# Sliding-window attention in chunks of 64 queries with 64x64 score tiles, instead of units of two heads and 128 queries

## The reference

```
CHUNK = 64; WINDOW = 128               # a chunk of queries sees its own chunk and the two before it
s = einsum('...lhgd,...mhd->...hglm', q, k) * HEAD_DIM ** -0.5
s = where(key_pos >= 0, s, -1e30)      # prompt: no keys ahead of the stream
p = softmax(concat([s, sink], -1))[..., :-1]      # one learned sink per head
a = einsum('...hglm,...mhd->...lhgd', p, v)
merged = concat([rms_norm(a, g_a), rms_norm(b, g_b), c]) @ w_out
```

## Time and profile before

| | us |
|---|---|
| median of 3 runs (lowest, highest) | 1426.18 (1425.39, 1429.57) |
| the profiled execution, own time | 1430.02 |
| its span, first to last instruction | 1428.0 |
| PE busy, share of the span | 1376.4, 96% |
| DVE busy | 688.4, 48% |
| ACT busy | 505.5, 35% |
| POOL busy | 213.1, 15% |
| mean granted TensorE clock | 0.982 |

### The profile page before, as it was taken

One profiled execution on the slowest core, in us unless ns is written; L12 is line 12 of the kernel. 1 busy time (PEld: TensorE's weight loads), 2 busy tenths in 40 slices (PEclk: granted clock), 3 DMA queues, 4 the chain that ended last, 5 costly groups with the idle time before them and its releaser, 6 DMA issues.

```text
span 1428.0 us, 24272 instructions
## 1 busy us (share of the span) xinstructions
PE 1376.4 (96%) x10358; PEld 1324.3 (93%) x10358; DVE 688.4 (48%) x1320; ACT 505.5 (35%) x1088; POOL 213.1 (15%) x257
## 2 busy tenths in 40 slices
PE   8999979999999999999999997899999999999996
PEld 8989858999999999999999896599999999999996
DVE  6556783555444444221458487717644444441213
ACT  4223374544232223222433125836532322232220
POOL 6502101520000000011343030124100000001110
PEclk9999988999999999999999999899999999999998
DMA  4412100213222222222222120002222222222211
GB/s 161 163 60 71 45 1 1 104 45 106 87 88 76 89 74 90 84 80 89 75 105 102 47 71 30 1 30 90 89 89 75 89 75 89 81 83 89 74 60 67
DMA packets 33643, 107.96 MB, mean 76 GB/s; under 512 B 4304, under 2 KB 8928, under 8 KB 33536
## 3 DMA queue, kind: packets, MB, share of 16 engines
q1 hardware_dynamic: 31056, 101.26, 20.7%
q0 software_dynamic: 2480, 5.15, 1.1%
HBM read 103.25 MB, written 3.15 MB: 75 GB/s over the span
## 4 chain that ended last, share of the span: by engine, by line
PE 80%; DVE 13%; issue 2%; ACT 2%; DMA 0%; POOL 0%; POOLq 0%; DVEq 0%; ACTq 0%
PE psum L449 25%; PE psum L451 24%; PE psum L450 24%; DVE h_lo L1238 2%; DVE mx L1487 1%; DVE w_lo L1231 1%; DVE x L1286 1%; PE psum L469 1%; PE psum L546 1%; DVE prob L1502 1%; DVE rsq L1373 1%; PE psum L745 1%; PE psum L459 1%; DVE h_whole L1515 1%; PE psum L570 1%
## 5 line engine op out<-in xcount | busy, mean ns | idle before, releaser
L449 PE MATMUL psum<-h_hi,w_hi 128*128 128x320 f32 (+1 forms) x2192 | 660.7, 301 | 5.2 <-DVE hid_whole L1275 3.1
L450 PE MATMUL psum<-h_lo,w_hi 128*128 128x320 f32 (+1 forms) x2192 | 651.2, 297 | 0.0
L451 PE MATMUL psum<-h_hi,w_lo 128*128 128x320 f32 (+1 forms) x2192 | 651.1, 297 | 0.0
L449 PEld LDWEIGHTS psum<-h_hi,w_hi 128*128 128x128 f32 x2192 | 417.5, 190 | 11.0 <-DVE hid_whole L1275 3.5
L450 PEld LDWEIGHTS psum<-h_lo,w_hi 128*128 128x128 f32 x2192 | 417.8, 191 | 2.2 <-issue 1.9
L451 PEld LDWEIGHTS psum<-h_hi,w_lo 128*128 128x128 f32 x2192 | 417.8, 191 | 0.0
L1231 DVE TENSOR_TENSOR w_lo<-raw,w_hi 128x1024 fp32r<-128x1024 f32 x184 | 232.1, 1267 | 337.7 <-ACT w_hi L883 337.6
L883 ACT ACTIVATE w_hi<-raw 128x1024 fp32r<-128x1024 f32 x184 | 192.4, 1050 | 177.1 <-DMA raw<-in_wts 176.8
L449 PE MATMUL psum<-hid_hi,w_hi 128*128 128x256 f32 (+1 forms) x672 | 198.1, 295 | 0.0
L451 PE MATMUL psum<-hid_hi,w_lo 128*128 128x256 f32 (+1 forms) x672 | 197.7, 294 | 0.0
L450 PE MATMUL psum<-hid_lo,w_hi 128*128 128x256 f32 (+1 forms) x672 | 197.7, 294 | 0.0
(11 more groups left out here) (173 smaller groups left out, 1227.1 us busy)
## 6 DMA issues: line engine op xcount, KB each, us to landing
raw<-in_wts SPq DMA_DIRECT2D x184, 512.0 KB, 3.2
tab<-in_tabs POOLq DMA_DIRECT2D x2, 642.0 KB, 4.9
x<-in_xT SPq DMA_DIRECT2D x2, 640.0 KB, 10.2
lp<-in_lpar POOLq DMA_DIRECT2D x2, 640.0 KB, 5.9
out_x<-x SPq DMA_DIRECT2D x4, 320.0 KB, 2.3
tab<-in_tabs POOLq DMA_DIRECT2D x2, 577.0 KB, 4.4
x<-in_xT SPq DMA_DIRECT2D x2, 512.0 KB, 5.3
out_x<-x SPq DMA_DIRECT2D x4, 256.0 KB, 2.1
```

Of the source, the lines that this page charges most:

```text
L449: pe.matmul(out, wh, hi, start=first, stop=False)
L450: pe.matmul(out, wh, lo, start=False, stop=False)
L451: return pe.matmul(out, wl, hi, start=False, stop=last)
```

## The change

Attention goes by 9 chunks of 64 queries, all eight heads at once. The 64 queries of heads j = 0 to 3 with both key heads fill 128 partitions and four column strips of `KW` = 192 keys. Keys are stored once, without zeros, and there is no mask: chunk 0 has 64 keys, chunk 1 has 128, the others 192 (`WINDOW`, `KEYS0`). Scores are 64x64 tiles at four positions of the array. V is kept in ten tiles (blocks that start at even and at odd chunks), so that each chunk takes one tile of 128 keys and one of 64. Turned probabilities are copied by ACT (`wideT`) and DVE (`halfT`).

```diff
-CYCLE = (0, 2, 6, 7, 1, 3)
+CYCLE = (2, 3, 0, 1, 7, 6)
+CHUNKS = T // CHUNK
+KEYS0 = [0, 0] + [CHUNK * (c - 2) for c in range(2, CHUNKS - 1)] + [SEQ]
+WINDOW = [(P, CHUNK), (0, P)] + [(0, P + CHUNK)] * (CHUNKS - 2)
-        prob = place("prob", [P, 4, 2, 256])
-        probT = place("probT", [P, 4, 2, 2, P])
+        prob = place("prob", [P, 2, 4, KW])
+        wideT = place("wideT", [P, 2, 4 * P])
+        halfT = place("halfT", [P, 2, 4 * P])
-        kk = place("kk", [P, 2, KC])
+        kk = place("kk", [P, KC])
+                fill[16].append(v_tokens)
...
# PE
+                def scores(c):
+                    o, n = WINDOW[c]
...
+                    elif c >= 2:
+                        pe.wait_ge(p_ready, L(c - 1, CHUNKS))
+                    for j in range(4):
+                        for h in (0, 1):
+                            r, at = slice(64 * h, 64 * h + 64), (j // 2) * KW + o
+                            mm = pe.matmul(banks[2 * (c % 2) + h][64 * (j % 2):64 * (j % 2) + 64, at:at + n],
+                                           qq[r, j, c * CHUNK:(c + 1) * CHUNK], kk[r, KEYS0[c]:KEYS0[c] + n],
+                                           start=True, stop=True, tile_position=(64 * h, 64 * (j % 2)))
+                def turn(c):
...
+                    pe.wait_ge(pn_ready, L(c + 1, CHUNKS))
+                    for j in range(4):
+                        if wide is not None:
+                            mm = pe.transpose(banks[4][:, j * P:(j + 1) * P], prob[:, c % 2, j, 0:P], ident[:, :])
+                        if half is not None:
+                            mm = pe.transpose(banks[5][0:CHUNK, j * P:(j + 1) * P], prob[:, c % 2, j, P:KW],
+                                              ident[:, :])
+                def values(c):
...
+                    for h in (0, 1):
+                        out = banks[6 + b % 2][64 * h:64 * h + 64, :].rearrange("p (j n) -> p j n", n=P)
+                        for i, (t, src, n) in enumerate(parts):
+                            probs = src[0:n, c % 2, 2 * P * h:2 * P * (h + 1)].rearrange("p (j q) -> p j q", q=CHUNK)
+                            mm = pe.matmul(out[:, :, at:at + CHUNK], vk[0:n, t, 64 * h:64 * h + 64], probs,
+                                           start=i == 0, stop=i == len(parts) - 1, tile_position=(0, 64 * h))
+                for c in range(CHUNKS + 2):
+                    if c < CHUNKS - 1:
+                        scores(c + 1)
+                    if 1 <= c < CHUNKS + 1:
+                        turn(c - 1)
+                    if c == CHUNKS + 1:
+                        part_out(0, bc, 4)
+                    if c >= 2:
+                        values(c - 2)
+                part_out(1, bc, 4)
...
+                sum_tokens(l, "a", 0, acc, 4, [(a_ssq, L(2, NB))])
+                part_out(2, bc, 4)
+                spread(l, "a", 0, 4)
+                part_out(3, bc, 4)
+                sum_tokens(l, "a", 1, acc, 5, [(a_ssq, L(NB, NB))])
+                part_out(4, bc, 8)
+                spread(l, "a", 1, 5)
+                part_out(5, bc, 8)
+                for i in range(4):
+                    part_out(i, a_, 12)
+                part_out(4, a_, 16)
+                part_out(5, a_, 16)
# ACT
+                more[16].append(lambda: preload(ACT.Exp))
+                more[17].append(vk_copy)
-                    if i > 1:
+                    if 1 < i < IN_T - 1:
                         split(L(S_IN + i - 1 + RING, SLOTS))
+                    for j in range(4):
+                        fn(prob[:, c % 2, j, o:o + n], score_at(c)[:, j // 2, j % 2, :], ACT.Exp,
+                           bias=nm[:, c % 2, j:j + 1], scale=SCALE, accum_out=den[:, c % 2, j:j + 1])
+                    fn(wideT[:, c % 2, :], banks[4], ACT.Copy).then_inc(pt_ready, 1)
+                for c in range(CHUNKS + 2):
+                    if c < CHUNKS:
+                        exps(c)
...
+                    if 1 <= c < CHUNKS + 1:
+                        turned(c - 1)
+                    if c >= 3 and c % 2:
+                        outs((c - 3) // 2)
+                    if 1 <= c <= EARLY:
+                        hi_of_merged(c - 1)
...
+                for n in (IN_T - 2, IN_T - 1):
+                    split(L(S_IN + n + RING, SLOTS))
# DVE
+                    dve.tensor_copy(halfT[0:CHUNK, c % 2, :], banks[5][0:CHUNK, :]).then_inc(half_ready, 1)
-                    for hh in (0, 1):
-                        last = dve.tensor_scalar(prob[0:n, u % 4, hh, 0:kn], prob[0:n, u % 4, hh, 0:kn],
-                                                 rd[0:n, u % 2, hh:hh + 1], None, ALU.mult)
+                    dve.tensor_tensor(prob[:, c % 2, :, o:o + n], prob[:, c % 2, :, o:o + n],
+                                      rd[:, c % 2, :].unsqueeze(2).to_broadcast([P, 4, n]), ALU.mult)\
+                       .then_inc(pn_ready, 1)
+                for c in range(CHUNKS + 2):
+                    if c < CHUNKS:
+                        maxima(c)
+                    if c >= 2:
+                        turned(c - 2)
+                    if 1 <= c < CHUNKS + 1:
+                        normalise(c - 1)
...
+                        merged(c - 1)
+                    if 2 <= c <= EARLY + 1:
+                        lo_of_merged(c - 2)
...
+                for n in (IN_T - 2, IN_T - 1):
+                    split(L(S_IN + n + RING, SLOTS))
                 split(L(S_OUT + RING, SLOTS))
# POOL
-                for hh in (0, 1):
-                    link(pool.memset(kk[64 - 64 * hh:128 - 64 * hh, hh, :], 0.0))
```

More of the change, by code:

```diff
@@ L726, in values @@
[L726 to L748, removed]
-                    mm.then_inc(o_done, 1)
@@ L751, in start_out @@
[L751 to L771, removed]
-                    if 3 <= u < UNITS + 3:
-                        turn(u - 3)
-                    if u >= 5:
-                        values(u - 5)
-                    if u in START_OUT:
-                        start_out(START_OUT[u])
-                    if u == A_AT:
-                        sum_tokens(l, "a", 0, acc, 7, [(a_ssq, L(2, NB))])
-                    if u == A_AT + 1:
-                        spread(l, "a", 0, 7)
@@ new lines, in values @@
+                def values(c):
+                    wide, half = VTILE[c]
+                    b, at = c // 2, c % 2 * CHUNK
+                    if c == 0:
+                        pe.wait_ge(ro_taken, L(NB, NB))
+                        pe.wait_ge(state_ready, L(NB, NB))
+                        pe.wait_ge(vk_ready, L(2, 2))
+                    elif c >= 4 and c % 2 == 0:
+                        pe.wait_ge(a_taken, L(b - 1, NB))
+                    pe.wait_ge(pt_ready, L(WIDE[c], WIDE[-1]))
+                    pe.wait_ge(half_ready, L(HALF[c], HALF[-1]))
+                    parts = [(t, src, n) for t, src, n in ((wide, wideT, P), (half, halfT, CHUNK)) if t is not None]
+                    for h in (0, 1):
[4 more added lines that the diff above has]
+                                           start=i == 0, stop=i == len(parts) - 1, tile_position=(0, 64 * h))
+                    mm.then_inc(o_done, 1)
@@ new lines, in part_out @@
+                def part_out(i, ks, ready):
+                    m, g = OUT_ORDER[i]
+                    pe.wait_ge(lo_made, L(S_OUT + m + 1, SLOTS))
+                    pe.wait_ge(h_ready, L(HR["merged"] + ready, HRS))
+                    for k in ks:
+                        mm = three(dense(i, g), L(S_OUT + m, SLOTS), k, h_hi[g][:, k, :], h_lo[g][:, k, :],
+                                   k == 4, k == 3)
+                    if 3 in ks:
+                        mm.then_inc(tile_done, 1)
@@ new lines, in _ @@
+                bc, a_ = range(4, KT), range(4)
+                scores(0)
+                v_new()
+                for c in range(CHUNKS + 2):
[8 more added lines that the diff above has]
+                part_out(1, bc, 4)
+                pe.wait_ge(pt_ready, L(WIDE[-1], WIDE[-1]))
```

301 lines of the change are left out of this document (129 added, 172 removed).

## The result

The changed kernel took 1384.74 us (median of 4 runs, 1384.46 to 1385.72), the kernel before 1427.38 beside it (4 runs, 1425.39 to 1429.57): a ratio of 0.9704, 95% interval 0.9689 to 0.9719. The forecast was 1384. The profiled execution took 1384.84 us at a span of 1382.9, which is 45.1 less than before's.

A forecast was written before the change was run, and what follows sets the result against it. DVE's chain of work was taken to bound the stage. First-layer stage 59.3 + 2.4 + 3 = 64.7 us; savings 22.2 + 20.0 = 42.2; profiled 1430.02 became 1387.8, less 3.8 for the median: 1384 us, range 1371 to 1408.

The forecast's parts named there:

- The prediction's 13 us of waits: Old first-layer loop: of 58.7 us, the 13 us left after DVE's units and merged pieces were called waits.
- DVE per chunk: DVE's work on a full chunk in the new loop: 1.26 + 0.61 + 1.28 + 0.87 = 4.0 us.
- PE per chunk: PE's scores, transposes and values of a chunk: 0.75 + 0.87 + 0.1 + 2.1 = 3.8 us.
- the three prices: A chunk's sixteen score matmuls: 0.65 us (all four tiles at once), 1.3 (column halves only) or 2.6 (no overlap).
- Splits and tables: Weight splits, Sqrt/Exp table switches and first-group normalisation leave the loop; moving the splits removes most of its listed waits.
- The loop, 39.2 us at full clock: First layer, from the first score matmul to the last values: 39.2 us, ending at 204.0.
- ACT's cover of 0.6 us: Behind odd chunks, ACT's exponentials queue after output copies with only 0.6 us to spare, showing first if PE is late.
- The two additions, 5.4 us: Added to the 59.3 us stage: 2.4 us for POOL slowing normalising and 3 us for a lower granted clock.
- The tail: Continuous PE work behind the loop, up to the seventh output tile: 7.8 + 9.3 + 2.9 = 20.0 us.
- PE as the bound: Rival, 17%: scores don't overlap or every switch costs more, so PE sets the turn; saving about 20 us, 1406.
- The clock low through the loop: Rival, 8%: PE at half clock takes 7.7 us a chunk and bounds the loop; 17 us slower, 1443.
- Nothing gained: Rival, 2%: the output stage waits for weights because it comes earlier; 1426 us.

The follow-up runs named there:

- splits behind: The kernel before with only the stage's two weight splits moved behind the loop over units: 1414.14 us, ratio 0.9920.
- the mask: The kernel before without its 32 mask matmuls a layer: 1426.52 us, ratio 1.0005.
- the reordered values: The changed kernel with value matmuls ordered by key tile, both column halves of one tile size side by side: 1379.71 us, ratio 0.9673.

## Why the prediction was right

**What bounds it.** DVE per query, as forecast. From the first score to the first output matmul the first layer took 58.7, 53.0 and 39.1 us (before, splits behind, changed) as DVE's busy time in the loop went 47.0, 44.2, 32.1: 15 us less work for DVE and some 5 us less of its idle time. In the new loop DVE's bound is shown: doubling its maxima cost nearly all of itself, doubling PE's scores little. In the old loop it is argued, from these lengths and from the mask, which cost PE time and not the loop. The prediction's 13 us of waits there were too many, since they held the two splits' own 2.5 us of work: DVE was idle for 11.7 us.

**DVE per chunk.** Forecast 4.0 us, measured 3.99. Maximum 0.95, half copy 0.68 (0.69), product 0.96 (0.97), pieces 0.55 and 0.48.

**PE per chunk.** Scores at the lowest of the three prices, all four tiles at once: sixteen more took 0.65 us. The row of the column halves was the right neighbour to go by. Values 2.29 instead of 2.1: a term sized 0.2 too low: by the same sum a switch of tile size costs, by an estimate, nearer 0.15 us than 0.1. The Trainium skill, TensorEngine Tiling (Key Properties), says that tiles of one mode run independently and that a change of mode drains; the scores agree with the first half, and the reordered values, 1.17 instead of 2.29 with half the changes of mode, agree with both.

**Splits and tables.** The splits and their waits are gone from the loop, worth 11.8 us by the medians in the kernel before (15.7 in its profiled stages). Two table loads alone were worth nothing where they were put back; the normalisation of the first token group in mid-loop, with its wait of PE, was not tried by itself.

**The loop, 39.2 us at full clock.** The second layer ran it at 1.00 in 42.48, so 3.3 more. The last product ends at 879.90, 35.1 us after the start, where the working had 32.65 (164.75 to 197.4): the waits behind ACT's output copies are 0.63 + 0.56 + 0.61 = 1.8 of the 2.5, the third chunk's maximum begins 0.6 later than summed (3.96 us after the start instead of 3.35), and two merged pieces beside POOL took 0.45 more; the turns between were a little shorter. What PE does behind it took 7.35 instead of 6.6: values 0.2 dearer twice, one part of an output tile 1.6 instead of 1.44. The prediction had called ACT's cover of 0.6 us the first to give way; it gave way at full clock, not only with PE late, and was priced at nothing. The working for the 0.6 cannot be followed as it stands: 9.4 plus 1.3 would be later than the 10 at which DVE asks.

**The two additions, 5.4 us.** Both were mis-sized. POOL: 2.4 us forecast, 0.45 measured in the second layer and under 0.1 in the first. POOL and then DVE in the second layer, the merged pieces while POOL worked:

```profile
857.95 1.18 POOL L1782 TENSOR_TENSOR acc<-sqa 128x128 f32<-128x128 f32 x1 [23.09 <-ACT sqa L885]
```

```profile
857.86 0.96 DVE L1509 TENSOR_TENSOR prob<-prob,rd 128x768 f32<-128x768 f32 x1
858.73 0.68 DVE L1522 SCALAR_TENSOR_TENSOR h_whole<-rT,sp,sg 128x256 f32<-128x256 f32 x1
859.34 0.67 DVE L1528 TENSOR_TENSOR h_lo<-h_whole,h_hi 128x256 fp32r<-128x256 f32 x1
```

The pieces slowed (0.48 and 0.42 elsewhere); the normalising products never took over 0.96, whereas the units' normalising had slowed to 1.17. Here DVE's product began 0.09 us ahead of POOL, and it was POOL's instruction that took 1.18 us, where the same one takes 0.45 to 0.46 at its other places in this loop. The clock: 3 us a layer forecast; the first layer had 7 us at 0.54 and its loop is 0.5 longer than the second's, which had none. So 64.7 was right to within 2.5 us (62.8 and 62.3) because 3.3 us of waits and dearer steps stood where 5.4 had been put: that they nearly cancel is luck.

**The time within 1 us.** This too is luck in part. The stages gave 46.5 us instead of 42.2, and 1.4 came back outside them, so the profiled executions differ by 45.1. But before's profiled execution, from which the saving was reckoned, lay 2.6 us above the median beside the changed kernel, and the changed kernel's lay at its own: the medians differ by 42.6. The forecast had taken its 42.2 from a median 3.8 us below that profiled execution.

**The tail.** Forecast 20.0 us, measured 19.8 in both layers, without a gap.

**The rivals.** PE as the bound: excluded for the changed kernel by the doubled scores and maxima, though PE's slack is small. The clock low through the loop: 0.92 and 1.00. The rule of the Trainium skill that spoke for it (TensorE: Matmul & The Clock Gate, Part 4: PE-mode transpose) did not decide here: the second layer's loop held the full clock with the transposes in it. Nothing gained: no wait of PE behind the seventh tile was new.

## What to carry to other kernels

Price the engine that the evenly running part of the chain goes through by work per result: wider instructions on it (768 columns instead of 512 and 256) paid, while the mask's matmuls, taken off a PE that was not the bound, did not. Count, too, what a single instruction from outside can do in a loop of engines that wait for each other: the same split cost 22.6 us (with its neighbour) where DVE came to it before ACT had its half and 6.7 one chunk later. And order matmuls by tile size, so that tiles of one size stand side by side.

## What the runs showed of the hardware that was not expected

- Two column halves of one tile size overlap, and alternating sizes loses that: eight 256-column value matmuls took 2.29 us with sizes alternating and 1.17 grouped.
- Two changes of ACT's table took 2.9 us, back to back. The Trainium skill, ScalarE: Activation LUTs (What ACT_TABLE_LOAD costs), gives about 2.66 us for each switch, 1.28 of it the load. The rows here show the 1.28 and no further idle time, so here two switches cost little more than one does by the page; the measurement decides.
- A low granted clock cost little where DVE set the turn: in the changed kernel's first layer 7 us at 0.54 stand in a loop 0.5 us longer than the second layer's at 1.00. Where PE was on the path it cost, by an estimate, about 3 us (half of the 7 us at 0.51 in the second layer of the reordered values).
- Which of two engines slows down beside the other can differ from case to case: in the one place of the changed loop where DVE's product had begun 0.09 us before POOL's sum, the product kept its 0.96 us and POOL's instruction took 1.18 instead of 0.45.
